# A two-block transformer kernel on one core: the order of GpSimd's row gathers and list stores at the start of the expert stage

## The reference

```python
logits = xf @ w_router + b_router                  # 512 tokens, 32 experts
top_val, top_idx = lax.top_k(logits, TOP_K)        # 4 experts per token
gates = jax.nn.softmax(top_val, axis=-1)
...
hu = xb @ w_up[e] + b_up[e]                        # rows xb of one expert e
x_glu = jnp.minimum(hu[:, :D_FF], SWIGLU_LIMIT)
x_lin = jnp.clip(hu[:, D_FF:], -SWIGLU_LIMIT, SWIGLU_LIMIT)
act = x_glu * jax.nn.sigmoid(SWIGLU_ALPHA * x_glu) * (x_lin + 1.0)
y = act @ w_down[e] + b_down[e]                    # D_FF = 1024, all float32
```

## Time and profile before

| | us |
|---|---|
| median of the three runs | 3534.59 |
| profiled execution, its own time | 3521.77 |
| span of the profiled execution | 3520.1 |
| PE busy | 3058.4 (87%) |
| vector engine (DVE) busy | 858.9 (24%) |
| scalar engine (ACT) busy | 499.0 (14%) |
| POOL busy | 236.1 (7%) |

### The profile page before, as it was taken

How to read it: one execution, slowest core, us unless ns; L and a number is a source line. 1 busy time by engine, 2 the same in 40 slices (tenths; PEclk the granted TensorE clock), 3 DMA queues, 4 the chain that set the end, 5 groups by cost and what they waited for, 6 DMA issues and landing times.

```text
span 3520.1 us, 36607 instructions
## 1 busy us (share of the span) xinstructions
PE 3058.4 (87%) x15338; PEld 1354.6 (38%) x15338; DVE 858.9 (24%) x1276; ACT 499.0 (14%) x983; POOL 236.1 (7%) x336
## 2 busy tenths in 40 slices
PE   7998878598999999999598899998799507999998
PEld 3465555232323333333246444444233203444443
DVE  2324242311211111111134300013320851201003
ACT  1031131000000000000013300002002930100001
POOL 0000011211011011011100000000100320000000
PEclk8989978799999999999799999999899758999999
DMA  7108941789999999999541212211220031312210
GB/s 263 48 7 306 358 139 41 289 321 404 389 403 406 400 401 404 404 402 391 232 168 44 82 48 95 94 67 53 57 65 25 14 71 30 113 48 95 85 58 24
DMA packets 167017, 646.18 MB, mean 184 GB/s; under 512 B 20091, under 2 KB 29883, under 8 KB 126257
## 3 DMA queue, kind: packets, MB, share of 16 engines
q1 hardware_dynamic: 151138, 605.91, 44.8%
q0 software_dynamic: 13872, 34.89, 3.4%
q10 hardware_dynamic: 1856, 3.21, 0.3%
HBM read 630.11 MB, written 18.38 MB: 184 GB/s over the span
## 4 chain that ended last, share of the span: by engine, by line
PE 49%; issue 32%; DMA 5%; DVE 5%; POOL 3%; PEld 2%; ACT 2%; POOLq 2%; DVEq 1%; PEldq 0%; ACTq 0%; SPq 0%
PE ps L2221 13%; PE ps L2232 13%; PE ps L2349 6%; PE ps L2525 3%; PE ps L2006 2%; DMA stage<-gate_dram 2%; DMA slots<-in_ada_w_dram 2%; PE ps L2171 2%; PE ps L1104 2%; POOLq L1536 2%; PE ps L314 1%; POOL work L1545 1%; PEld ps L434 1%; PE ps L245 1%; DVE slots L2494 1%
## 5 line engine op out<-in xcount | busy, mean ns | idle before, releaser
L1645 PE MATMUL ps<-slots,hT 128*32 128x512 f32 x5120 | 581.4, 599 | 25.8 <-issue 9.4
L2221 PE MATMUL ps<-hT,slots 128*128 128x512 f32 x1024 | 448.6, 599 | 13.1 <-issue 6.6
L2232 PE MATMUL ps<-slots,work 128*128 128x512 f32 x1024 | 441.8, 593 | 12.2 <-DVE work L2269 12.2
L1645 PEld LDWEIGHTS ps<-slots,hT 128*32 128x32 f32 x5120 | 160.8, 110 | 422.4 <-issue 407.2
L2221 PEld LDWEIGHTS ps<-hT,slots 128*128 128x128 f32 x1024 | 195.1, 192 | 265.7 <-issue 265.7
L2232 PEld LDWEIGHTS ps<-slots,work 128*128 128x128 f32 x1024 | 193.7, 190 | 258.8 <-issue 247.6
L1681 PE MATMUL ps<-slots,work 128*32 128x512 f32 x2112 | 253.7, 606 | 27.8 <-DMA slots<-in_w_down_dram 20.0
L2349 PE MATMUL ps<-hT,slots 128*96 128x512 f32 x512 | 223.3, 597 | 26.6 <-DVEq L2355 24.8
L2525 PE MATMUL ps<-slots,work 96*128 96x512 f32 x256 | 112.6, 602 | 107.2 <-DVE work L2512 107.2
L1796 DVE TENSOR_SCALAR stage<-ps 128x512 f32<-128x512 f32 (+1 forms) x47 | 32.2, 686 | 589.3 <-PE ps L1647 588.9
L1681 PEld LDWEIGHTS ps<-slots,work 128*32 128x32 f32 x2112 | 90.2, 111 | 158.6 <-issue 126.6
(11 more groups left out here) (542 smaller groups left out, 2891.8 us busy)
## 6 DMA issues: line engine op xcount, KB each, us to landing
slots<-in_w_up_dram SPq DMA_DIRECT2D x128, 2048.0 KB, 18.0
slots<-in_w_down_dram SPq DMA_DIRECT2D x64, 2048.0 KB, 16.4
slots<-in_mlp_w_dram SPq DMA_DIRECT2D x32, 2048.0 KB, 8.7
slots<-in_ada_w_dram SPq DMA_DIRECT2D x16, 2048.0 KB, 9.5
slots<-in_w_ada_dram SPq DMA_DIRECT2D x12, 2048.0 KB, 8.3
slots<-in_ada_w_dram SPq DMA_DIRECT2D x16, 1024.0 KB, 7.1
slots<-in_rnn_w_in_dram SPq DMA_DIRECT2D x8, 1536.0 KB, 7.1
slots<-in_w_in_dram SPq DMA_DIRECT2D x5, 2048.0 KB, 13.1
```

The source lines that it names most:

```text
L1645: ins = pe.matmul(to, x[:, k, unit * UNIT:(unit + 1) * UNIT], upw[s][:, k % 2, col:col + CH], start=k == 0, stop=False)
L2221: ins = pe.matmul(ps[:, m], slots[:, s, k, m * P:(m + 1) * P], hT[:, k, :], start=k == 0, stop=k == KT - 1)
L2232: ins = pe.matmul(ps[:, 4 + 2 * (t % 2) + h], h1T[:, k, t * P:(t + 1) * P], slots[:, 2 + h, k], start=k == 0, stop=k == KT - 1)
```

## The change

Only POOL's program is changed. The gather of pass 2, ahead of which the wait for `route_step` 6 stays, and the gather of pass 3 come first, and the list stores move into the loop over passes: two at the head of each of the first eight passes, ahead of the gather of pass i + 4. The wait for the list's first fill (`list_filled`) moves to just ahead of the loop, and one settle less is issued, since the gather's own settle stands behind `route_step` 6.

```diff
             moe_gather(g, 0)
             g.wait_ge(S("biases"), 1)
             moe_gather(g, 1)
-            g.wait_ge(S("list_filled"), 16)
             g.wait_ge(S("route_step"), 6)
-            settle(g)
-            for j in range(TT * TOPK):
-                g.indirect_dma_start(list_dram, bass.IndirectOffsetOnAxis(ap=sloti[:, j:j + 1], axis=0),
-                                     pairs[:, 3 * j:3 * j + 3], None, bounds_check=E * T - 1, oob_is_err=False).then_inc(S("list_out"), 16)
             moe_gather(g, 2)
             g.wait_ge(S("blocks_listed"), 1)
             moe_gather(g, 3)
+            g.wait_ge(S("list_filled"), 16)
             for i in range(NPASS):
+                for j in range(2 * i, min(2 * i + 2, TT * TOPK)):
+                    g.indirect_dma_start(list_dram, bass.IndirectOffsetOnAxis(ap=sloti[:, j:j + 1], axis=0),
+                                         pairs[:, 3 * j:3 * j + 3], None, bounds_check=E * T - 1, oob_is_err=False).then_inc(S("list_out"), 16)
                 if i + 4 < NPASS:
                     moe_gather(g, i + 4)
                 for q, units, at in quads(i):
```

## The result

| | before | changed |
|---|---|---|
| median of the runs, us | 3533.22 (7 runs, 3519.53 to 3539.7) | 3513.65 (7 runs, 3502.94 to 3518.41) |
| ratio of the times, 95% interval | | 0.9943 (0.9924 to 0.9962) |
| profiled execution: span, own time | 3520.1, 3521.77 | 3512.0, 3513.65 |
| first pass's up product starts (to there: gate, router) | 651.75 | 657.12 |
| from there to the third pass's up product: the **interval** | 64.33 | 53.99 |

The change is faster by 0.57%, 19.6 us, with 13 to 27 us by the interval of the ratio.

The account below looks back on a forecast made before the run. TensorE, busy 87% of the span, was taken as the bound, so POOL's change pays only where PE stands still. Hole -8.62 and clock -2.2 gave -10.8 us, from a median of 3534.59 to 3523.8 us, range 3518 to 3538.

Parts of the forecast that it names:

- The gather goes ahead, cost nothing: Third pass's gather ahead of the list stores on POOL: rows landed by 680.2 us, 12 us before need; cost 0.
- at most 8.62 us: PE's hole in the second pass's up product, blamed on the store burst: gain 0 to 8.62 us, taken as 8.62.
- Clock, 2.2 us: Second pass's last 96 matmuls at full clock without the hole: 12.80 to 10.58 us, gain 2.2, bounds 0 and 2.2.
- Weights, no new wait: Third pass's up weights load earlier along with the freed slots; long product starts at 705.3 us, added wait 0.
- Pairs of stores, nothing: Two stores in each of eight passes add 2.55 us each to POOL, hidden in its 532.2 us of waiting; cost 0.
- Moving from the profiled execution to the median: Whole kernel: median taken as 12.8 us above the profiled execution, so forecast 3511.0 us becomes 3523.8 us.
- the hole stays: Rival: PE's hole has another cause, returns, or belongs to the profiled execution alone; no change, 3534.6 us within 2; chance 0.34.
- Slower, since each pair holds PE: Rival: PE's drains are held during each of eight store pairs, 5 us each; 3564 us, or 3543.8 for half; chance 0.08.

Follow-up runs that it names:

- experiment 1: Kernel before and changed kernel, both unchanged, profiled and timed again on chip 14: before against itself 0.9997, changed 0.9954 (3516.98 against 3531.41 us).
- experiment 5: Kernel before with some stores moved behind the fourth pass's gather, or without the settle behind all sixteen; chip 1: eight ahead 0.9975 (3520.51 us), no settle 0.9991.

## Why the prediction was wrong

Its sign was right and its size too small by 9 us. By its own steps:

1. *The gather goes ahead, cost nothing.* Right as to cost: the rows landed at 685.7 us, forecast 680.2 at most on a clock that ran 5.4 us earlier, so within 0.2 us of it. But the step gave no gain to it, since in the profile at hand the rows "land about 1 us before PE asks for them". That is the same place where the next step fails.
2. **The step that failed: "at most 8.62 us".** The hole of one profiled execution was taken for what the stores cost in every execution, and was made the upper bound of the gain. In the three further profiles of the kernel before the hole was absent and PE waited 14.89 to 15.85 us for the third pass's rows. The text had the piece in its hand: it saw that rows and hole "come out at the same place". It even said that with the hole alone gone "PE would wait for the rows instead". But it priced that with the rows of the disturbed profile, and its rival let the other executions wait for less. The rows did not stay where that profile had them: the hole had emptied the DMA engines, and that gave the short settle (2.43 us at a share of 0.01, against 6.20 to 7.04 at 1.02). Without it the last row landed 57.0 us behind the first product's start (experiment 1), not 51.4, and PE asked for it after 42.1 us: a wait of 14.9. A delay that stands in another's shadow has to be priced anew when that other is gone.
3. *Clock, 2.2 us.* Right in kind, and too large for the hole: the second product took 5.55 + 12.80 = 18.35 us with the hole and 17.01 without, 1.3 us less. Its last 96 matmuls take 11.13 us at a granted clock of 1.00 (688.10 to 699.23 in the changed kernel on chip 9), not the 10.58 worked out from the long product, and at its start the clock is low in the changed kernel too (0.59 from 681.59 to 686.90). With the hole's 8.62 us and 0.4 us ahead of the product that makes the 10.3 us between the two first profiles. Against the wait for rows the clock adds this: the granted clock was 0.62 in the wait of experiment 1. Behind it the down product took 8.60 us where it takes 7.38, and the third pass's transposes 3.02 where they took 2.7 in the changed kernel: 1.5 us. 14.9 + 1.5 = 16.4 = 70.39 - 53.99.
4. *Weights, no new wait.* Right. The long product was to start 705.3 - 651.75 = 53.6 us after the first one; it starts after 53.99, and in the other profiles of the changed kernel after 53.98 to 54.61.
5. *Pairs of stores, nothing.* Right as far as the profiles tell: the rest of the passes is 2.45 us longer in the first pair of profiles, but within the spread of the others; POOL's wait is 533.7 against 532.2, the vector engine's two waits 8.6 and 7.7 against 8.5 and 7.0. That a store beside vector work "is not longer in this trace" was read from means, and they hide it. In that trace one store took 1.07 us and one gather 1.25, where 0.97 is usual, and both lie beside the vector engine's L1805:

```profile
674.52 1.07 POOL L1573 DMA_INDIRECT list_dram<-pairs,work  x1 [0.30 <-issue]
```

From 655 to 1150 us of all twenty profiles every issue of a store or a gather above 1.06 us, up to 1.47, lies beside that instruction, which reads two SBUF tiles. It adds 0.5 us at most. The Trainium skill's figure of about 3100 ns (SBUF — State Buffer, "A bandwidth-pool intuition that's wrong (but worth ruling out)") was seen nowhere, but the changed kernel's stores hardly test it: of the sixteen, three touch a vector instruction at all, 0.97 us each.
6. *Moving from the profiled execution to the median* by the constant 12.8 us carried the error of step 2 along. The forecast end of the interval was right, its start was not: 64.33 us where the others have 70.4, that is 6.1 of the 9 us. The other 3 us lie inside the spread of the medians.

By the profiles the gain is 70.39 - 53.99 = 16.4 us, inside the measured 13 to 27. So the step that failed is the price of the stores' delay: 8.62 us at most in the prediction, 14.9 us of waiting for rows in the runs.

The rivals: that *the hole stays* and nothing is gained is wrong, yet its reserve, that the hole belongs to the profiled execution, was the point; it assumed that the others would wait less, and they waited longer. *Slower, since each pair holds PE* is wrong: of the changed kernel's four profiles none has a drain over 4.6 us. Its mechanism, for a whole burst, is one reading of chip 9, where a burst beside the second pass made the kernel slower than before; it isn't shown. The Trainium skill's sentence (SBUF — State Buffer, "Who interferes with whom") that PE never waits on anyone of the shared port is not contradicted as such, since no run shows what links the held drains to POOL.

## What to carry to other kernels

Before a gap of one profile is priced, profile the kernel again: here one profile showed a hole of 8.6 us and three others a wait of 15 us for another thing. Where two delays come out at the same place, work out each one's time with the other gone, and with the transfer queues as full as they then are. Issue what a later pass will wait for ahead of a run of small indirect transfers, each of which holds GpSimd's queue for 1.27 us, and spread the run: on two chips that cost and gained nothing beyond the spread, and on chip 9 the spread order was the only one of four without a long stall.

## What the runs showed of the hardware

- GpSimd's settle (a tiny add and a drain) was short where the DMA engines were idle. Behind sixteen indirect stores it took 6.28, 6.20 and 7.04 us in the kernel before at a DMA share of 1.02, and 2.43 and 2.55 us at 0.01, where a stall had stopped the weights. Between pairs of stores it took 5.0 to 5.8 us at a share of 0.82 or more and 1.84 us at 0.01.
- The three row gathers of the third pass, 256 KB each, landed 7.8 to 10.1 us after their issue in the four profiles of the changed kernel and 8.8 to 11.8 us in the three profiles of the kernel before without a hole, both beside the weight stream. With fewer stores or no settle ahead of them (experiment 5, chip 1) it was 5.3 to 13.1 us.
- The issue of an indirect DMA on GpSimd (a list store or a row gather) took 0.9 to 1.06 us, and more, up to 1.47 us, only beside a vector instruction that reads two SBUF tiles.
- On two of five chips (and in the first profile) TensorE stood 2.4 to 13.1 us at a time with no releaser named, beside a burst of GpSimd's stores or the settle behind it, and in one profile hand-overs to the scalar engine took up to 3 us. Bursts in the same places showed none of it on the three other chips.
- The changed kernel and the one that moves only the third pass's gather lay 17 us apart on chip 9 (3514.72 and 3531.55 us). On chip 1 the latter gained 20 us over the kernel before (3510.53 against 3531.06).
